# Modulation pieces one step ahead of the key and value products, and eight filling steps ahead of the first scores instead of four

## The reference

```
mod = einsum('bd,de->be', silu(c), w_mod) + b_mod
sh1, sc1, g1, sh2, sc2, g2 = split(mod, 6)
hc = modulate(rmsnorm(ctx, norm1_g), csh1, csc1)      # k_ctx, v_ctx = hc @ w_in[kv columns]
hx = modulate(rmsnorm(x, norm1_g), sh1, sc1)          # modulate(h, s, c) = h * (1 + c) + s
q_x, k_x, v_x, u_x, b_x, c_x, ga_x, gc_x = split_projection(hx @ w_in)
q, k = apply_axial_rope(q_x), apply_axial_rope(k_x)
o_attn = latent_window_attention(q, k, v_x, k_ctx, v_ctx, sink)   # 4 query blocks, softmax with a sink
y_conv = short_conv_mixer(u_x, b_x, c_x, conv_w)
```

## Time and profile before

| | |
|---|---|
| median of three runs | 2009.65 us |
| lowest and highest | 2007.29, 2009.83 us |
| the profiled execution's own time | 2013.01 us |
| its span | 2011.3 us |
| mean granted clock of TensorE | 0.969 of full |
| TensorE busy with products | 1889.6 us (94% of the span) |
| VectorE, ScalarE, GpSimd busy | 962.5, 656.7, 77.9 us |
| memory read | 345.53 MB |

### The profile page before, as it was taken

The page is one execution under the profiler, slowest core; times in us unless marked ns, Lnnn a source line. Parts: engine busy times, 40 slices in busy tenths (PEclk is TensorE's granted clock), DMA queues, the critical chain, the costliest instruction groups (busy, mean ns, idle before and its releaser), DMA issues.

```text
span 2011.3 us, 23356 instructions
## 1 busy us (share of the span) xinstructions
PE 1889.6 (94%) x9685; PEld 1384.4 (69%) x9691; DVE 962.5 (48%) x1620; ACT 656.7 (33%) x1134; POOL 77.9 (4%) x70
## 2 busy tenths in 40 slices
PE   6999998999999699999999799999898999999998
PEld 4777777778878434344433389897676778888886
DVE  4788777752553422231322244524454557636643
ACT  4445444442242401020110144223545443212333
POOL 0101000000000000000000000002121200000000
PEclk9999999999999799999999999999897999999999
DMA  9324333252343399999999932351211323243231
GB/s 322 115 74 126 99 111 95 85 179 93 112 156 138 147 414 421 421 421 422 421 421 421 362 118 69 100 171 43 63 42 63 126 84 100 68 136 100 65 98 42
DMA packets 176540, 355.14 MB, mean 177 GB/s; under 512 B 7122, under 2 KB 148530, under 8 KB 151090
## 3 DMA queue, kind: packets, MB, share of 16 engines
q1 hardware_dynamic: 172688, 338.85, 45.7%
q10 hardware_dynamic: 3458, 14.50, 2.0%
q0 software_dynamic: 288, 0.30, 0.1%
HBM read 345.53 MB, written 8.39 MB: 176 GB/s over the span
## 4 chain that ended last, share of the span: by engine, by line
PE 78%; DVE 8%; ACT 5%; DMA 4%; POOL 2%; issue 2%; SPq 0%; ACTq 0%; DVEq 0%; POOLq 0%
PE ps L484 75%; PE ps L487 2%; POOL tb L2783 1%; DMA rx<-in_w_exp_up 1%; DMA rx<-in_w_exp_down 1%; ACT M L1236 1%; DVE small L2124 1%; DMA md<-in_w_mod 1%; ACT k2h L1236 1%; DVE wsp0l L1875 1%; DVE X L1884 1%; POOL MH L2783 1%; ACT KR L1236 0%; DMA M2b<-m_spill 0%; DVE acc L1884 0%
## 5 line engine op out<-in xcount | busy, mean ns | idle before, releaser
L484 PE MATMUL ps<-H,wsq1h 128*128 128x512 f32 x640 | 202.4, 398 | 7.3 <-DVE tb L1875 4.1
L484 PE MATMUL ps<-H,wsq0h 128*128 128x512 f32 x608 | 194.0, 401 | 4.6 <-DVE tb L1875 4.5
L484 PE MATMUL ps<-rx,XE 128*64 128x512 f32 x752 | 176.4, 600 | 2.2 <-DMA rx<-in_w_exp_up 2.2
L484 PE MATMUL ps<-H,wsp1h 128*128 128x512 f32 x544 | 174.3, 402 | 0.1
L484 PEld LDWEIGHTS ps<-H,wsq1h 128*128 128x128 f32 x640 | 121.2, 192 | 33.4 <-DVE tb L1875 4.5
L484 PEld LDWEIGHTS ps<-H,wsq0h 128*128 128x128 f32 x608 | 116.4, 193 | 31.2 <-DVE tb L1875 5.8
L484 PE MATMUL ps<-H,wsp0h 128*128 128x512 f32 x368 | 124.2, 416 | 8.0 <-ACT H L1236 8.0
L484 PE MATMUL ps<-H,wsq1l 128*128 128x512 f32 x320 | 126.2, 395 | 0.0
L1875 DVE TENSOR_TENSOR wsq1l<-ring,wsq1h 128x1024 fp32r<-128x1024 f32 (+2 forms) x72 | 77.6, 1119 | 99.8 <-ACT wsq1h L1236 99.8
L484 PE MATMUL ps<-H,wsq0l 128*128 128x512 f32 x304 | 120.5, 397 | 0.0
L484 PEld LDWEIGHTS ps<-H,wsp1h 128*128 128x128 f32 x544 | 100.7, 192 | 21.1 <-issue 2.1
(11 more groups left out here) (372 smaller groups left out, 3568.0 us busy)
## 6 DMA issues: line engine op xcount, KB each, us to landing
rx<-in_w_exp_gate SPq DMA_DIRECT2D x49, 1024.0 KB, 16.3
rx<-in_w_exp_down SPq DMA_DIRECT2D x46, 1024.0 KB, 19.7
rx<-in_w_exp_up SPq DMA_DIRECT2D x45, 1024.0 KB, 18.0
ring<-in_w_in SPq DMA_DIRECT2D x39, 1024.0 KB, 5.3
ring<-in_w_up SPq DMA_DIRECT2D x20, 1024.0 KB, 5.2
ring<-in_w_exp_up SPq DMA_DIRECT2D x19, 1024.0 KB, 19.6
ring<-in_w_mod SPq DMA_DIRECT2D x18, 1024.0 KB, 7.2
ring<-in_w_exp_down SPq DMA_DIRECT2D x18, 1024.0 KB, 17.9
```

Of the source, the lines that this page charges most:

```text
L484: return pe.e.matmul(o, l, r, start=start, stop=stop, skip_group_check=True)
```

## The change

It does three things. On TensorE each piece of modulation from 2 to 7 is now wrapped around one block of products: its raw products stand ahead of the block and its sum behind it, and the blocks are keys 0, keys 1, values 0, keys 2, keys 3, values 1. Behind them come keys 4 and 5, values 2, keys 6 and 7. On VectorE the order follows: for each block n from 0 to 5 the norm of n, the row of piece n + 2, the low parts of n, and the output of piece n + 2. The low part of the value slab is made behind the output of piece 3. And `early_units` becomes 8.

```
-    early_units, units = 4, 4 * 7 + 8 * 12
+    early_units, units = 8, 4 * 7 + 8 * 12
...
-        keys(0)
-        for c in (1, 3, 5):
-            mod_raw(c + 1)
-            keys(c)
-            mod_sum(c + 1)
-            mod_raw(c + 2)
-            values_of(c // 2)
-            mod_sum(c + 2)
-            keys(c + 1)
+        for j, products, c in ((2, keys, 0), (3, keys, 1), (4, values_of, 0), (5, keys, 2), (6, keys, 3), (7, values_of, 1)):
+            mod_raw(j)
+            products(c)
+            mod_sum(j)
+        keys(4)
+        keys(5)
+        values_of(2)
+        keys(6)
         keys(7)
...
         for c in range(0, 8, 2):
-            norm_x(c)
-            norm_c(c)
-            left_x(c)
-            norm_x(c + 1)
-            left_c(c)
-            norm_c(c + 1)
-            left_x(c + 1)
-            left_c(c + 1)
-            if c < 6:
-                mod_row(c + 2)
-                if c == 0:
+            for n in (c, c + 1):
+                norm_x(n)
+                norm_c(n)
+                if c < 6:
+                    mod_row(n + 2)
+                left_x(n)
+                left_c(n)
+                if c < 6:
+                    mod_out(n + 2)
+                if n == 1:
                     lo(slabs["v"])
-                mod_out(c + 2)
-                mod_row(c + 3)
-                mod_out(c + 3)
```

## The result

The changed kernel takes 1997.22 us, the median of four runs (1995.67 to 2000.06), against 2009.74 (2007.29 to 2014.64) of the kernel before on the same chip: ratio 0.9936, 95% interval 0.9922 to 0.9950.

The account below looks back on a forecast made before the run. TensorE, busy 94% of the span, was taken to bound the kernel. Terms 9.1 - 2.8 - 1.0 = 5.3 us off the 2009.65 us median gave 2004.4 us; range 1999.5 to 2011.5, or 2001.5 to 2007 by its bounds alone.

Parts of the forecast that it names:

- Part 1: First keys to query slab: modulation pieces one ahead remove TensorE's waits, query slab at 67.6 instead of 76.72; gain 9.1 us.
- the rival of weights: Ahead of the query slab: modulation waits become waits for weights, so no gain there; 2013.5 us, chance 0.05.
- Part 2: First to second scores: eight early steps delay the softmax, second scores 8.4 us later for steps worth 5.6; loss 2.8 us.
- The rule on GpSimd: Second query slab's rotation: VectorE and GpSimd block each other, GpSimd ends 0.5 us later; would give 2004.9, left out of sum.
- Part 3: Attention: moved steps add 4.4 us idle, moved query-slab turnovers give 3.4 back; loss 1.0 us, bounds 5.6 loss, 3.4 gain.
- idle in iterations 2, 10, 18, 26: Attention transposes: TensorE comes 1.4 us earlier, ScalarE doesn't; up to 5.6 us new idle, taken as 4.4.
- iteration 14: Attention: fourth query slab's rotation moves out of the transposes' way; their wait could fall from 2.26 to 0.25 us.
- iteration 22: Attention: the query slab's turnover comes one step earlier; the transposes' wait could fall from 5.68 to 4.3 us.
- The rest from 480 us on: Stage untouched by the change, taken as rigid: earlier gains reach the end one for one; over 2 us change means wrong.
- Nothing is given back: Second scores and attention: softmax's extra VectorE work is owed either way, so no losses there; 2000.5 us, chance 0.15.
- The attention turns the gain into a loss: Iterations 2, 10, 18, 26: full 1.4 us idle plus 1.65 at half clock each, 12.2 us; 2015.5 us, chance 0.12.
- The clock rival: Value wait and 98.45 us: clock falls behind the new waits too, two falls costing 3.3 us; 2007.7 us, chance 0.20.

Follow-up runs that it names:

- experiment 8: Changed kernel with a step put back in each of iterations 2, 10, 18 and 26 and taken out two iterations later; 2001.85 us, ratio 0.9952.
- experiment 1: Kernel before with only early_units raised from 4 to 8, modulation order as before; 2006.58 us, ratio 0.9987.
- experiment 4: Changed kernel with four of the eight early steps moved behind the first scores, to the end of iteration 0; 1993.9 us, ratio 0.9922.
- 7: Changed kernel with four early steps behind the first scores, block 1 normed early, value low part halved, turnover in iteration 21; 1991.73 us, ratio 0.9915.
- 9: Changed kernel with four early steps behind the first scores, block 1 normed early and value slab's low part in halves; 1988.47 us, ratio 0.9883.
- experiment 2: Changed kernel with early_units back at 4, so the new modulation order alone; 2000.17 us, ratio 0.9956.
- experiment 3: Changed kernel with the 116 later steps at the places of the kernel before, only iteration 31 left without; 1997.94 us, ratio 0.9941.
- 6: Changed kernel with two more steps in iteration 21, one taken from 22 and one from 24; 1998.35 us, ratio 0.9943.
- 10: Changed kernel with six steps ahead of the first scores instead of eight; 2003.61 us, ratio 0.9966.

## Why the prediction was wrong, step by step

**Part 1, gain 9.1: right.** The query slab starts at 67.63, forecast 67.6. That is partly luck, since the first keys came 0.54 us later in this execution; the stage itself went from 43.77 to 34.14, 9.6 us. The new waits were 1.00 (forecast 1.1) and 1.42 us (forecast 1.9). The order alone gave 9.6 us in the medians. No load was late: the two new waits, 2.42 us, are all that TensorE idled from 33.49 to 67.63 (31.72 busy of 34.14). So the rival of weights fell.

**Part 2, loss 2.8: right.** From the query slab to the second scores it took 8.46 us more for four steps of 5.6: a loss of 2.9. Split of the ninth slab 1.37 (forecast 1.4), second scores 106.59 (106.6), wait 4.72 (4.6).

**The rule on GpSimd, half borne out.** Around the rotation of the second query slab the changed kernel has two modulation steps beside both halves (timeline of VectorE and GpSimd):

```profile
94.42 1.30 POOL L2778 TENSOR_TENSOR tb<-tb,cst 128x512 f32<-128x512 f32 x1 [11.55 <-DVE tb L2013]
94.83 2.60 DVE L1883 SCALAR_TENSOR_TENSOR acc<-ring,cT,acc 128x256 f32<-128x256 f32 x2
...
95.80 1.35 POOL L2778 TENSOR_TENSOR tb<-tb 128x512 f32<-128x512 f32 x1
97.84 1.39 DVE L1883 SCALAR_TENSOR_TENSOR KR<-tb,tbr 64x512 fp32r<-64x512 f32 x2 [0.42 <-ACT tbr L1235]
```

The pair took 2.60 us, where two of them without GpSimd took 1.00 (107.36 in the same trace). GpSimd took 2.73 from start to end, against 2.61 in the kernel before (103.52 to 106.13). So VectorE was held for 1.6 us, and GpSimd ended 0.1 later, not 0.5. The hold cost the chain nothing, since `query_lo` behind it (97.84) still had 0.42 us to wait for ScalarE's copy. The Trainium skill (SBUF — State Buffer, Who interferes with whom) has the two block each other, and says that the order of issue decides which of them waits. In this trace GpSimd's instruction had started first both times, 94.42 against 94.83 and 95.80 against 96.03 for the second step of the pair, and the hold lay almost wholly on VectorE. That agrees with the order of issue; the forecast had used only that the two block each other. The 0.5 us by which the rule would have made the gain smaller (2004.9) doesn't show in the trace.

**Part 3, loss 1.0: the step that failed.** By it the stretch from the second scores to the last sums should have taken 315.33 less 5.6 plus 1.0, 310.7 us; it took 304.26. This one term is 6.5 us, where forecast and median are 7.2 apart. Idle times of TensorE over 0.15 us from iteration 2 on add up to 18.7 us before and 15.4 after, and windows of 1 us from behind the second scores (109 and 108) to 480 us give 8.9 and 6.9 us lost at half clock:

| term | forecast | measured |
|---|---|---|
| idle in iterations 2, 10, 18, 26 | +4.4 | +1.2 (0.25, 0.30, 1.50, 1.80 to 0.25, 0.79, 0.99, 3.03) |
| iteration 14 | -2.0 | -1.9 |
| iteration 22 | -1.4 | -1.7 |
| iterations 6, 16, 28 | not seen | -2.4 (0.98, 0.43, 1.24 to 0.25, 0, 0) |
| iterations 5, 8 | not seen | +1.4 |
| stretches at half clock | not seen | -2.0 |

So the step that failed is this one term, in two ways: the emptied places were charged 4.4 us where 1.2 more stood in the profile, and the waits of the other iterations and the stretches at half clock, 3.0 us of gain together, were put at nothing.

The prediction's reading of the table was also incomplete. Besides the places that it names, `upto` takes a step behind the scores out of iterations 5, 13, 21 and 29. By number, these four are the steps that now stand ahead; those of iterations 2, 10, 18 and 26 only move on to 4, 12, 20 and 28.

The forecast's sentence was "TensorE comes to the transposes 1.4 us earlier, while ScalarE isn't earlier", less the slack there is. Experiment 8 differs from the changed kernel in these places alone and tests it. The four iterations idle 0, 0.5, 0.7 and 1.4 us more without their step than with it. What differs among them is ScalarE's slack and its work in front of the copies. ScalarE in iteration 2 of the kernel before, from the end of the exponentials:

```profile
123.21 0.19 ACT L1236 ACTIVATION_READ_ACCUMULATOR M<-ps,small 128x1 f32 x1
123.30 0.58 ACT L1236 ACTIVATE tb<-ps 128x512 f32<-128x512 f32 x1
123.78 1.15 ACT L1236 ACTIVATE wsp1h<-ring 128x512 fp32r<-128x512 f32 x2
124.82 0.27 ACT L1236 ACTIVATE A<-ps 128x128 f32<-128x128 f32 x1
125.44 1.51 ACT L1236 ACTIVATE M<-ps 128x512 f32<-128x512 f32 x3 [0.35 <-PE ps L487]
```

In the changed kernel:

```profile
122.20 0.20 ACT L1235 ACTIVATION_READ_ACCUMULATOR M<-ps,small 128x1 f32 x1
122.42 0.28 ACT L1235 ACTIVATE A<-ps 128x128 f32<-128x128 f32 x1
123.00 1.51 ACT L1235 ACTIVATE M<-ps 128x512 f32<-128x512 f32 x3 [0.30 <-PE ps L487]
```

And in experiment 8, which has the step there again:

```profile
122.19 0.28 ACT L1235 ACTIVATE A<-ps 128x128 f32<-128x128 f32 x1
124.20 1.51 ACT L1235 ACTIVATE M<-ps 128x512 f32<-128x512 f32 x3 [1.74 <-PE ps L487]
```

The copy into `tb` and the two half splits, 1.7 us, are gone from this place in both, with the step and without it. They belong to other steps: with four more done ahead, other steps fall into iteration 2. So ScalarE had 1.74 us of slack there, enough for the 1.4 us by which TensorE comes earlier, and the iteration went from 10.16 to 8.70 us, the full worth of a step. In iteration 26 it is the other way. ScalarE has the same rows in front of the copies in the changed kernel and in experiment 8, the copy into `tb` among them, and the wait at the third pair is longer by all of the step (TensorE's timeline, changed kernel, then experiment 8):

```profile
355.22 0.44 PE L487 MATMUL ps<-cst,M 128*128 128x128 f32 x2 [2.01 <-ACT M L1235]
```

```profile
357.30 0.44 PE L487 MATMUL ps<-cst,M 128*128 128x128 f32 x2 [0.59 <-ACT M L1235]
```

Iterations 10 and 18 lie between. In 18 the step brings a copy into `tb` of 0.60 us on ScalarE with it (274.88 in experiment 8, none in the changed kernel), so there, and in none of the other three, it is as experiment 8 expected, that a part of ScalarE's work goes with the step. The forecast's mechanism is thus borne out in iteration 26 and costs nothing in iteration 2; what it had wrong was the slack, for which it read TensorE's timeline of the kernel before alone. Against the kernel before the four iterations cost only 1.2 us, since 18 and 26 waited 1.50 and 1.80 us there already. ScalarE's order in the new kernel could have been written down beforehand.

The half clock lost in before's stretch from 365 to 369 us (4 us at 0.58, 1.7 us) stood behind iteration 26's 1.80 us wait. The changed kernel shows no such stretch behind 3.03 us of waits there. In this profiled execution it is a gain; experiments 1, 4, 7 and 9, with the same two waits there, do show one, of 1.5 to 1.7 us. So it can't be credited to the change as a sure gain.

**What stays open.** With eight early steps done by the second scores the attention takes 302.8 to 305.5 us, with four 314.5 and 315.3, in all twelve such kernels, wherever the rest stands, and 309.9 with six. Some 3.4 to 7 us of that are beyond the steps' own worth. Part of this is the clock. Take the time lost at half clock from each stage, as an estimate the stage times one less its mean granted clock (9.4 us before, 7.2 in the changed kernel, 5.1 in experiment 4). Then both kernels with four steps took 306.0 us, those with eight ahead of the first scores 295.9 to 297.3, and those with four of the eight behind them 298.3 to 300.4. Beyond the steps' 5.6 us the first group of eight wins 3.1 to 4.5, and the second only 0 to 2.1: much of what the attention wins is the other side of the loss at the first scores. The table above says where the 5.5 us of the changed kernel lie. Why the waits' sum goes with the number of steps left, while single waits move with the table, was not settled; that the softmax has less to share ScalarE and VectorE with is argued only.

**The rest from 480 us on: rigid in the work, not to 2 us.** The stage from 480 to 1000 us has the same 492.20 us of busy time. Behind the last sums the two profiled executions differ by 3.8 us (TensorE busy 1510.66 and 1503.79 us at 0.97 and 0.98) with alike programs, and the thirteen kernels spread from 1582.5 to 1589.8. Taken at the medians, 1997.22 and 2009.74 less what lies around the spans (1.7) and the last sums (411.66, 423.36), the two come to 1583.9 and 1584.7: no difference.

**The forecast's range.** The bounds that the prediction gives for part 3, 5.6 us of loss and 3.4 of gain, would make 2000.0 to 2009.0 with parts 1 and 2 as they stand, and not its own range of 2001.5 to 2007. The measured time lies below both.

**The rivals.** "Nothing is given back" (2000.5) was nearest, but for another reason: part 2's loss was there, and the attention paid for it. "The attention turns the gain into a loss" had the sign wrong, since waits elsewhere did get shorter. The clock rival did not occur in the profiled execution, at 1.00 from 33.49 to 67.63, but see below.

## What to carry to other kernels

When a step is taken from a place, write down what every engine then has in front of the wait, in the new order, and how much slack it has there, before charging anything: the same 1.4 us cost 0, 0.5, 0.7 and 1.4 us of wait at four places. Work put ahead of a first dependent product is better put behind it, where that product's consumer is waited for anyway: the same eight steps cost 6.6 us less there, of which the attention took 1.1 back. And in a table of places, a long wait that is moved away tends to stand elsewhere afterwards; compare the length of the whole stage, not the one wait.

## What was not expected of the hardware

The clock did not follow the waits from one execution to the next. Seven kernels (changed, 2, 3, 4, 6, 8, 10) have the same program up to the query slab, with the same waits of 1.0 and 1.42 us. In five of their profiled executions the clock stayed at full; in 3 and 6 it fell behind the second wait, which made the stage 1.5 us longer (35.60 and 35.62 against 34.10 to 34.14). Windows of the changed kernel and of experiment 3:

```profile
44.00:48.00 4.00, 4.00 (x40) 3.19 (x40) 3.81 (x10) 1.68 (x3) 0.00 (x0) 1.00 1.15 307
```

```profile
44.00:48.00 4.00, 4.00 (x25) 3.98 (x29) 2.35 (x5) 1.13 (x2) 0.00 (x0) 0.57 1.17 306
```

Behind the long waits it was no surer. In the kernel before it fell behind all three waits of 1.98 us and not behind the 2.09 ahead of the first keys. Experiment 1 has the same program there, and in its profiled execution the clock fell behind the 2.10 ahead of the first keys (34.87) and behind two of the three waits of 1.98, but not behind the one at 61.22. And the 2.97 us ahead of the second scores, at half clock in the kernel before, had no fall in experiment 2 (1.00 from 94 to 102 us). The windows of experiment 1:

```profile
35.00:39.00 4.00, 4.00 (x20) 2.89 (x24) 3.20 (x6) 2.85 (x5) 0.00 (x0) 0.59 0.96 309
61.00:65.00 4.00, 3.78 (x30) 2.62 (x31) 3.70 (x7) 1.81 (x4) 0.00 (x0) 1.00 0.00 0
```

The forecast's argument against the clock rival, that the 2.09 had no fall behind it, was thus worth less than it looked. One profiled execution can show a fall that the next of the same program doesn't have, and a difference of a few us between two profiles may be that alone.
